# A second attention whose far keys are multiplied residue by residue, two query blocks weighed together

## What is computed

```
D_ATT, ATT_HEAD_DIM, ATT_STEPS, DILATIONS = 1024, 64, 128, (1, 4, 16)   # 16 heads
def dilated_window_attention(q, k, v, slopes, dilation):
    # query t attends to t - j*dilation, j = 0..ATT_STEPS
    ...
    scores = jnp.where(valid, q.k - slope * distance, -inf)
    lse = logsumexp(scores); o = softmax(scores) @ v
o1, l1 = dilated_window_attention(q, k, v, slopes, 1)
o2, l2 = dilated_window_attention(q, k, v, slopes, 4)
o3, l3 = dilated_window_attention(q, k, v, slopes, 16)
wts = softmax([l1, l2, l3])
y_att = wts[0]*o1 + wts[1]*o2 + wts[2]*o3      # then gated by silu(z_att) and normalised
```

## Time and profile before

| | us |
|---|---|
| median of three runs | 2180.79 |
| the profiled execution | 2177.81 |
| its span, first to last instruction | 2175.8 |
| TensorE busy (matmuls) | 2021.0 (93%) |
| VectorE busy | 1216.0 (56%) |
| ScalarE busy | 807.1 (37%) |
| GpSimd busy | 615.2 (28%) |

### The profile page before, as it was taken

The page is one execution under the profiler, slowest core; times in us unless marked ns, Lnnn a source line. Parts: engine busy times, 40 slices in busy tenths (PEclk is TensorE's granted clock), DMA queues, the critical chain, the costliest instruction groups (busy, mean ns, idle before and its releaser), DMA issues.

```text
span 2175.8 us, 27306 instructions
## 1 busy us (share of the span) xinstructions
PE 2021.0 (93%) x10756; PEld 1023.9 (47%) x10756; DVE 1216.0 (56%) x2334; ACT 807.1 (37%) x1347; POOL 615.2 (28%) x630
## 2 busy tenths in 40 slices
PE   2999889998999999989998999999999999999896
PEld 2443344454344555434444665444555555555542
DVE  6419999899994555223455778300434443444616
ACT  2413444332314865123222444311444444434503
POOL 0022416452636002778112223212012022202240
PEclk8999999999999999999999999999999999999998
DMA  8110111112331011324111002011011101110301
GB/s 329 39 48 22 47 39 50 59 43 73 126 117 49 20 49 69 145 78 155 58 39 39 1 1 78 1 44 73 1 39 40 40 1 40 40 40 1 117 20 77
DMA packets 18383, 127.62 MB, mean 59 GB/s; under 512 B 1744, under 2 KB 1744, under 8 KB 13008
## 3 DMA queue, kind: packets, MB, share of 16 engines
q1 hardware_dynamic: 12720, 97.57, 12.0%
q0 software_dynamic: 5536, 28.31, 3.3%
HBM read 107.01 MB, written 18.87 MB: 58 GB/s over the span
## 4 chain that ended last, share of the span: by engine, by line
PE 78%; DVE 11%; ACT 4%; POOL 3%; DMA 2%; issue 2%; SPq 0%; DVEq 0%; POOLq 0%; ACTq 0%
PE ps L855 49%; PE ps L852 7%; PE ps L909 5%; PE ps L894 5%; PE ps L927 4%; DVE arena L1543 3%; POOL arena L544 2%; PE ps L1112 1%; PE ps L1132 1%; PE ps L977 1%; DMA W<-in_mods 1%; POOL arena L675 1%; ACT arena L1386 1%; DVE arena L1823 1%; DMA arena<-gates_scratch 1%
## 5 line engine op out<-in xcount | busy, mean ns | idle before, releaser
L855 PE MATMUL ps<-hT,W 128*128 128x512 bf16 x3456 | 812.1, 389 | 16.3 <-ACT arena L1231 6.3
L855 PEld LDWEIGHTS ps<-hT,W 128*128 128x128 bf16 x3456 | 323.1, 97 | 468.3 <-issue 29.6
L553 POOL TENSOR_TENSOR W<-W 128x512 bf16<-128x512 f32 x216 | 235.8, 1130 | 463.0 <-DMA W<-in_loads 461.7
L855 PE MATMUL ps<-W,arena 128*128 128x512 bf16 x1152 | 262.2, 388 | 8.5 <-DVE W L1877 6.6
L1556 DVE COPY arena<-ps 128x512 f32<-128x512 f32 (+3 forms) x302 | 156.4, 558 | 197.1 <-PE ps L927 189.5
L1569 DVE CUSTOM_DVE_ANT_0 arena<-ps,arena 128x128 f32<-128x128 f32 (+7 forms) x192 | 138.4, 755 | 191.5 <-PE ps L909 171.1
L1313 ACT ACTIVATE arena<-arena,small 128x128 f32<-128x128 f32 (+7 forms) x192 | 147.3, 768 | 185.5 <-DVE small L1569 185.3
L544 POOL TENSOR_TENSOR arena<-arena 128x512 f32<-128x512 f32 (+1 forms) x80 | 141.6, 1770 | 193.8 <-ACT arena L1480 124.7
L1320 ACT ACTIVATE arena<-arena,small 128x128 f32<-128x128 f32 (+7 forms) x192 | 138.4, 768 | 126.4 <-DVE small L1580 126.4
L855 PEld LDWEIGHTS ps<-W,arena 128*128 128x128 bf16 x1152 | 110.7, 96 | 158.3 <-DVE W L1877 7.1
L927 PE MATMUL ps<-ck,arena 128*128 128x128 f32 x864 | 124.9, 277 | 20.1 <-DVE arena L1556 13.3
(11 more groups left out here) (299 smaller groups left out, 2241.6 us busy)
## 6 DMA issues: line engine op xcount, KB each, us to landing
W<-in_loads SPq DMA_DIRECT2D x34, 2048.0 KB, 8.1
gates_scratch<-arena SPq DMA_DIRECT2D x32, 256.0 KB, 2.0
arena<-gates_scratch POOLq DMA_DIRECT2D x2, 4096.0 KB, 15.5
arena<-in_x SPq DMA_DIRECT2D x2, 2048.0 KB, 13.9
W<-in_mods SPq DMA_DIRECT2D x2, 2048.0 KB, 18.5
hT<-in_mods SPq DMA_DIRECT2D x2, 2048.0 KB, 29.0
arena<-in_x POOLq DMA_DIRECT2D x1, 4096.0 KB, 13.7
x_scratch<-arena POOLq DMA_DIRECT2D x8, 512.0 KB, 10.4
```

The costliest lines, as they stand in the source:

```text
L553: last = nc.gpsimd.tensor_tensor(low(v), v, high(v), ALU.subtract)
L855: last = mm(o, left[:, :, a], right[:, :, b], start=(k == 0 and (a, b) == PRODUCTS[0]), stop=(k == steps - 1 and (a, b) == PRODUCTS[-1]))
```

## The change

The eight q columns' evacuation writes queries within each block of 128 in the order of their residue mod 4 (`RES`), 32 (`RUN`) of each. The keys of an item are then two parts. Near: the block itself and the one before, 256 keys (128 at i = 0), multiplied as before (L963). Far: of all keys before the block every fourth, separately for each residue: 32 queries as weights, 64 rows, into 32 PSUM partitions, 32i columns read with a step of four elements, eight matmuls (four residues, two heads) for an item with i >= 2 (L969). The row of weights of an item is 32i + 256 wide instead of 128(i+1), at most 480. The last 32 far keys lie in the near block and are masked.

The turn (L986, L989) transposes two near blocks and the far part in chunks of up to 128 columns; a chunk of 64 columns (i = 2, 3, 6, 7) makes a tile of 64 output partitions. Weighing (L1018, L1024, L1031) is done for two items at once, after the odd one: the block near to both with 256 moving columns, one block each, and for each chunk of far keys and each residue a matmul of 2x32 columns. For it, v is also turned residue by residue (L1002) into `pair_far`, beside the plain turn (L1006); both now stand in the attention, for pair 0 too, and the two units L826 are gone from the 16 turns. Scores have two sets of banks and wait for the bias of item n-2. `close2` takes two blocks with a permuted access that puts tokens back in order. The bias tables are 480 wide instead of 1024, and both halves of them now lie in `pk`. ScalarE's exp and scale, VectorE's bias and copies run on the narrower rows.

```diff
+
+RES = 4
+RUN = P // RES
+FAR = 7 * RUN
...
-        TB = [area(28672 + 1024 * x, 1024) for x in range(2)]
-        dist = pk[:, PARAMS["br"].start:PARAMS["ci"].stop]
-        nlog = area(30720, 1024)
+        TB = [area(28672 + 512 * x, WINDOW) for x in range(2)]
+        dist, nlog = (pk[:, PARAMS["br"].start + WINDOW * n:PARAMS["br"].start + WINDOW * (n + 1)] for n in range(2))
...
                    cols=[[area(28160 + 512 * (2 * s + x), 512) for x in range(2)] for s in range(2)])
-        at2 = dict(rows=[[area(22528 + 1024 * (2 * s + x), 1024) for x in range(2)] for s in range(2)],
-                   cols=[[area(26624 + 512 * (2 * s + x), 512) for x in range(2)] for s in range(2)])
+        at2 = dict(rows=[[area(22528 + 512 * (2 * s + x), 512) for x in range(2)] for s in range(2)],
+                   cols=area(26624, 2048, "p (s x c) -> p s x c", s=2, x=2))
...
-        V_TURNED_AT = [8 * j + 5 for j in range(7)]
-        groups1, groups2 = groups_of(items1), groups_of(items2, V_TURNED_AT)
+        groups1 = groups_of(items1)
...
+        def far_keys(i):
+
+            return RUN * i if i >= 2 else 0
+
+        def far_turned(i):
+
+            return RUN * (i - i % 2) if i >= 2 else 0
+
+        def window(i):
+
+            return far_keys(i) + P * min(i + 1, 2)
+
+        def near_place(i, back):
+
+            return (i + 1 + back) % 2
+
+        V_TURNS = {0: (0, "far"), 1: (0, "near")}
+        for j in range(1, 8):
+            V_TURNS[8 * j - 2], V_TURNS[8 * j - 1] = (j, "far"), (j, "near")
+
+        item_group, v_group, groups_made = {}, {}, []
+        count = 0
+        for n in range(len(items2) + 2):
+            if 1 <= n <= len(items2):
+                item_group[n - 1] = count
+                count += 1
+            if n in V_TURNS:
+                v_group[n] = count
+                count += 1
+            groups_made.append(count)
...
-            pool.wait_ge(s_att[1]["transposed"], 2 * groups2[-1][-1][0] + 2)
+            pool.wait_ge(s_att[1]["weighted"], 32)
...
+            def window_attention(sems, items, filler):
+
+                def scores(n):
+
+                    j, i = items[n][3], items[n][2]
+                    if i == 0:
+                        pe.wait_ge(s_free, FIRST[f"pair{j}"] + 4)
+                    if n >= 2:
+                        pe.wait_ge(sems["biased"], 2 * (n - 1))
+                    q, k = pair_q[j % 2], pair_k[j % 2]
+                    far = far_keys(i)
+                    for x in range(2):
+                        last = mm(ps[:, 2 + 2 * (n % 2) + x, far:window(i)], q[halves[x], i * P:(i + 1) * P],
+                                  k[halves[x], max(i - 1, 0) * P:(i + 1) * P], start=True, stop=True)
+                    if far:
+                        for r in range(RES):
+                            for x in range(2):
+                                at_ = i * P + RUN * r
+                                last = mm(ps[RUN * r:RUN * r + RUN, 2 + 2 * (n % 2) + x, 0:far],
+                                          q[halves[x], at_:at_ + RUN], of_residue(k[halves[x]], r, 0, far),
+                                          start=True, stop=True)
+                    last.then_inc(sems["scores"], 1)
+
+                def turn(m):
+
+                    i, g = items[m][2], item_group[m]
+                    far, near = far_keys(i), min(i + 1, 2)
+                    for x in range(2):
+                        rows_ = at2["rows"][m % 2][x]
+                        pe.wait_ge(sems["scaled"], 2 * m + x + 1)
+                        if g >= 1:
+                            pe.wait_ge(sems["copied"], 2 * g - 1 + x)
+                        for back in range(near):
+                            b = near_place(i, back)
+                            at_ = far + (near - 1 - back) * P
+                            last = nc.tensor.transpose(ps[:, 6 + x, b * P:(b + 1) * P], rows_[:, at_:at_ + P], ident)
+                        for c in range(0, far_turned(i), P):
+                            n = min(P, far_turned(i) - c)
+                            last = nc.tensor.transpose(ps[0:n, 6 + x, 2 * P + c:3 * P + c], rows_[:, c:c + n], ident)
+                        last.then_inc(sems["transposed"], 1)
+
+                def turn_v(n):
+
+                    (j, what), g = V_TURNS[n], v_group[n]
+                    pe.wait_ge(s_free, FIRST[f"pair{j}"] + 6)
+                    for c in range(2):
+                        if g >= 1:
+                            pe.wait_ge(sems["copied"], 2 * g - 1 + c)
+                        for q in range(4):
+                            if what == "far":
+                                keys = 2 * RUN if c else 4 * RUN
+                                last = nc.tensor.transpose(ps[0:keys, 6 + c, q * P:(q + 1) * P],
+                                                           of_residue(pair_vT[j % 2], q, P * c, keys), ident)
+                            else:
+                                t = 4 * c + q
+                                last = nc.tensor.transpose(ps[:, 6 + c, q * P:(q + 1) * P],
+                                                           pair_vT[j % 2][:, t * P:(t + 1) * P], ident)
+                        last.then_inc(sems["transposed"], 1)
+
+                def weigh(m):
+
+                    i, j = items[m][2], items[m][3]
+                    pe.wait_ge(sems["copied"], 2 * groups_made[m + 1])
+                    if m >= 2:
+                        pe.wait_ge(sems["read"], m // 2)
+                    o = ps[:, 1, 0:2 * P]
+                    for x in range(2):
+                        mm(o[halves[x]].rearrange("p (s q) -> p s q", s=2), pair_v[j % 2][:, i - 1, DH * x:DH * x + DH],
+                           at2["cols"][:, :, x, P:2 * P], start=True, stop=False)
+                    for q in range(2):
+                        k = i - 2 + 2 * q
+                        for x in range(2):
+                            if k >= 0:
+                                last = mm(o[halves[x], P * q:P * q + P], pair_v[j % 2][:, k, DH * x:DH * x + DH],
+                                          at2["cols"][:, q, x, 0:P], start=False, stop=(i == 1))
+                    for c in range(0, far_turned(i), P):
+                        n = min(P, far_turned(i) - c)
+                        for r in range(RES):
+                            for x in range(2):
+                                at_ = 2 * P + c + RUN * r
+                                last = mm(o[halves[x]].rearrange("p (s q) -> p s q", s=2)[:, :, RUN * r:RUN * r + RUN],
+                                          pair_far[j % 2][0:n, c // P, r, DH * x:DH * x + DH],
+                                          at2["cols"][0:n, :, x, at_:at_ + RUN], start=False,
+                                          stop=(c + P >= far_turned(i) and r == RES - 1))
+                    last.then_inc(sems["weighted"], 1)
+
+                for n in range(len(items) + 2):
+                    if n < len(items):
+                        scores(n)
+                    filler(n, 0)
+                    if n >= 3 and n % 2:
+                        weigh(n - 2)
+                    if 1 <= n <= len(items):
+                        turn(n - 1)
+                    filler(n, 1)
+                    if n in V_TURNS:
+                        turn_v(n)
...
-                        last = A(pair_q[j % 2][:, span], bank, ACT.Copy, scale=-ATTN_SCALE)
+                        last = A(pair_q[j % 2][:, span].rearrange("p (t r s) -> p t r s", t=4, r=RES),
+                                 bank.rearrange("p (t s r) -> p t r s", t=4, r=RES), ACT.Copy, scale=-ATTN_SCALE)
...
+            def window_attention(sems, items, bias_of, close, extra):
+
+                def copies(m):
+
+                    i, g = items[m][2], item_group[m]
+                    for x in range(2):
+                        dve.wait_ge(sems["transposed"], 2 * g + x + 1)
+                        if m >= 2:
+                            dve.wait_ge(sems["weighted"], m // 2)
+                        to = at2["cols"][:, m % 2, x]
+                        far = far_turned(i)
+                        if far % P == 0:
+                            cols = slice(0 if i else P, 2 * P + far)
+                            V.tensor_copy(to[:, cols], ps[:, 6 + x, cols]).then_inc(sems["copied"], 1)
+                        else:
+                            whole = 2 * P + far - far % P
+                            V.tensor_copy(to[:, 0:whole], ps[:, 6 + x, 0:whole])
+                            V.tensor_copy(to[0:far % P, whole:whole + P], ps[0:far % P, 6 + x, whole:whole + P])\
+                                .then_inc(sems["copied"], 1)
...
+                for n in range(len(items) + 2):
+                    if n < len(items):
+                        i = items[n][2]
+                        dve.wait_ge(sems["scores"], n + 1)
+                        if n >= 2:
```

(33 more changed lines are left out.)

147 lines of the change are left out of this document (57 added, 90 removed).

## The result

The changed kernel takes 2130.84 us (median of 4 runs, 2128.42 to 2132.96), beside 2180.42 us for the kernel before in the same session: a ratio of 0.9772, 95% interval 0.9755 to 0.9789.

The account below looks back on a forecast made before the run. TensorE, busy 93% of the span, bounds the kernel. Six pairs -22.8, first -1.9, 16 turns -0.9, last pair -10, bias tables -1.2: -37 from 2177.8 gives 2140.8, plus 3.0 for the median 2143.8 us; range 2131 to 2168.

Parts of the forecast that it names:

- far scores: TensorE's new far score matmuls in one pair: tiles side by side, 2.9 us for the six items, the low end.
- weighing: TensorE's weighing in one pair: from 10.8 to 6.3 us, far passes paced by loading their 64-wide weights; -4.5 us.
- turning: Transposes in one pair: 7.8 us before, then 5.0 plus 2.2 for tile size changes around eight 64-wide ones; -0.6 us.
- bank 0: The gate that frees this bank stands behind copies of v at items 6 and 7: +1.6 us a pair, plus 0.3.
- rival A: Far scores' reads with a step of four cost: half rate 1.3 us a pair, 2154; a quarter, 2177; chance 0.20.
- Rival D: The small far score tiles do not overlap: +10 us for each of eight pairs, 2224 us; chance 0.06.
- B: Transposes into 64 partitions, far ones and those of v, take two passes: +10 us, 2154; chance 0.06.
- C: In the full pairs the ring of engines takes over from TensorE and the gain is gone: 2175 to 2185; chance 0.06.
- The first pair: First pair of the attention: also takes the plain turn of v and its own far turn, +1.9; net -1.9 us.
- The last pair: Pair without filler, set by the ring of engines: 49.8 to 40 us, -10; smaller bias tables another -1.2.
- 3.7 are a wait for GpSimd's sum of squares: In the last pair, 3.7 of 49.8 us wait for GpSimd's sum; closing item 0 one item later removes it.
- About 2 us are matmuls at half clock: In the last pair, about 2 of 49.8 us are matmuls at half clock behind that idle time; counted as gain.

Follow-up runs that it names:

- the run with full turns: Changed kernel with the far chunks of 64 columns turned 128 wide like all others: 2134.62 us, 67.79 us a pair.
- the run with 32 columns: Changed kernel with the two blocks of an odd item weighed one after the other, 32 moving columns instead of 64: 2156.93 us, 70.07 us a pair.
- The slower ring: Changed kernel with one more ScalarE copy of a row tile in each of the last pair's eight items: 2134.2 us, last pair 39.07 us.

## Why the prediction was off

**Direction and main mechanism were right**, the size was short by a quarter. TensorE was the bound; the change took 1.4 us a pair more from it than I summed. By the prediction's own steps, for one pair of the changed kernel:

| step | forecast, us | measured, us |
|---|---|---|
| near scores | 4.8 | 5.0 |
| far scores | 2.9 | 3.95 |
| weighing | 6.3 | 6.0 |
| turning | 7.2 | 5.24 |
| two turns of v | 2.0 | 1.95 |
| bank 0 | 1.9 | 1.21 |
| sum | 25.1 | 23.4 |

- **Turning is the step that failed.** "Eight of them are 64 columns wide in their own tile size, between full ones: in and out, 8 x 0.27 = 2.2." The 0.27 came on top of 0.108 for the transpose itself; the trace has 0.11 for both together, and the run with full turns shows no difference. I had taken 0.09 us from the earlier trace rows for a change of tile size as such. There the group that follows is another sort of work. Between transposes a change of columns costs nothing; a change from 128 to 64 rows in the weighing costs 0.10 us. The sum priced seven pairs this way (the last one went by the ring), and 2.0 us in each are 14 us: more than the whole miss of 12.6.
- **Far scores: the low end was right about the tiles and wrong about the step.** Eight side by side take 2.44 us with plain reads, 0.5 less than the forecast; their starts are 7 ns apart where I had 13, a figure that the earlier trace rows, at 30 ns an instruction, did not give. The read at step four adds 1.51 us, 1.15 of it seen by the pair, 8 in seven pairs. This is rival A at its half rate, priced at 1.3 us a pair and +10 in all. It happened, at 0.20 of chance, and was hidden in the total by the turning. Rival D fell, and so did B (the transposes into 64 partitions in two passes) and C (the ring in the full pairs: TensorE is busy 66.5 of 67.8 us and no filler waits for ScalarE).
- **Weighing was right** in size, and the moved columns indeed do not set its pace. The Trainium skill's rule in "TensorE: Matmul & The Clock Gate", "Part 3: Packing small matmuls — row/col tiling", that a load overlaps only across row groups, would have made it 1.8 us more. The trace gives 6.0 us, and the run with 32 columns shows that the streams lie beside whatever sets the pace.
- **Bank 0**: the wait at item 0 was forecast as 1.2 us and is 1.21. Its 0.4 at item 7 did not come, since the slow reads make the scores of item 7 0.4 us longer and cover it; with plain reads it is there, 0.36. The 0.3 for item 1 was 0.13, which the table has under near scores.
- The rest of the pair: these steps are 1.7 us under the forecast, the pair 1.4. In the kernel before the same steps take 29.1 us from start to start where I had 28.9, and the sixteen half units of filler, which I took as unchanged, went from 43.9 to 44.4.
- **The first pair** -3.2 (forecast -1.9), with the same two errors. **Ahead of it** -2.6 (forecast -0.9); the later runs show such differences in code that is the same, and I take nothing from it.
- **The last pair** -12.4, forecast -11.2 with the bias tables: near in its sum by luck, wrong in its parts. "3.7 are a wait for GpSimd's sum of squares": taking it away in the kernel before gave 0.8, not much more than the 0.6 by which two profiles of one kernel differ there (37.40 and 36.83). "About 2 us are matmuls at half clock": a price of that size is borne out (about 2.4 in the changed kernel), but the change did not take the half clock away. The granted clock is 0.90 of 49.83 us before and 0.86 of 37.40 after, which is 5.0 and 5.2 us of full clock lost. So of 5.7 us some 0.8 came, and narrower rows with less work for TensorE (its busy time fell from 39.58 to 29.51 us) brought some 11.6, where I had 5.7 and no term for TensorE's work. The slower ring shows it open for some six tenths; how the 11.6 divide between ring and TensorE was not separated.
- **The range** was too narrow downwards. Its low end let the last pair and the bank waits vary, but held the turning term for certain, though its one source was a row of another stage.

## What to carry to other kernels

- A price read off as "the next group starts 0.09 us late" belongs to that pair of groups. Ask what changed between them (rows, columns, a semaphore) before it is multiplied by eight.
- Here a float32 moving read kept nearly its full rate at step 2 and half of it at step 4. Where an order by residue is wanted, let an idle engine make a copy of it, from SBUF and not from the bank that the next unit waits for.
- Where the trace names one releaser, the next in line may be close behind it (here 1.2 us, of a wait of 3.7). Look at the other engines' queues in the same microseconds before the wait is counted as gain.
- Where an engine has several things to do, the one that frees a bank on which TensorE waits should come first: it was worth 1.0 us a pair.
- Where the granted clock differs between two executions, compare stretches in which it is the same, and not whole pairs.

## What the runs showed of the hardware that I had not expected

- Float32 moving reads: 0.83 ns a column and pass at step 1, 0.91 at step 2, 1.76 at step 4, with eight tiles side by side.
- Eight tiles of 64 rows by 32 columns start 7 ns apart, in whichever order of heads and residues they are issued.
- Float32 transposes of 64 columns stand 0.109 us apart from those of 128, each one instruction (other float32 matmuls are two), at no cost for the change. The Trainium skill, page "TensorEngine Tiling (Array Packing)", section "Restrictions and Gotchas", excludes such transposes with column tiles; in this kernel they run and cost like the others.
- In the weighing, with float32 weights 64 wide and 128 rows, an instruction starts every 26 to 28 ns, for 32 moving columns as for 64: the streams lie beside what sets the pace.
- Behind the same wait of 2.37 us the clock fell to half in one execution and not in another; 32 matmuls of L1031 then took 2.06 us against 1.25, and the stretch up to the last turn 31.09 us against 30.11, though TensorE waits in it for a ring of engines. Behind the last turn the same instructions took 4.85 us at full clock and 7.22 at a granted clock of 0.53.
